# Projections with the split activations streamed side by side: 512-column and 256-column matmuls in place of three of 256

## What is computed

```python
def conv_ffn(h, w_in, conv_w, conv_b, w_out):        # w_in 2048 x 11264, w_out 5632 x 2048
    u = h @ w_in
    u = conv_general_dilated(u, conv_w, causal, depthwise, width 3) + conv_b
    x1, x2 = jnp.split(u, 2, axis=-1)
    return (gelu(x1) * x2) @ w_out

# in rwkv7_time_mix, each of the three weights 2048 x 2048
    r = xr @ w_r
    k = xk @ w_k
    v = xv @ w_v
```

## Time and profile before

| | |
|---|---|
| median of 3 executions | 3236.29 us (3229.45 to 3247.82) |
| span of the profiled execution | 3236.4 us |
| up projection of the first ConvFFN | 508.6 us |
| up projection of the second ConvFFN | 508.8 us |
| r, k, v projections | 95.1, 93.9 and 95.0 us |
| pieces of weights made (all phases) | 792 |

### The profile page before, as it was taken

The page is one execution under the profiler, slowest core; times in us unless marked ns, Lnnn a source line. Parts: engine busy times, 40 slices in busy tenths (PEclk is TensorE's granted clock), DMA queues, the critical chain, the costliest instruction groups (busy, mean ns, idle before and its releaser), DMA issues.

```text
span 3236.4 us, 69175 instructions
## 1 busy us (share of the span) xinstructions
PE 2869.6 (89%) x27134; PEld 2794.3 (86%) x27134; DVE 2113.4 (65%) x2599; ACT 1468.9 (45%) x1994; POOL 151.8 (5%) x160
## 2 busy tenths in 40 slices
PE   2399999899999999985999677778788999999998
PEld 2399998899999998975999677667688999999998
DVE  6777777866666666678453598989537666665434
ACT  0143333466666633338453232322245666665333
POOL 0000000000000000000000221221000000000000
PEclk8599999899999999997999888989899999999999
DMA  8788788655555578872565444545344555555553
GB/s 298 250 280 278 273 275 283 234 180 183 182 181 181 182 242 279 289 225 73 162 194 169 145 145 151 161 132 166 112 146 144 181 181 181 182 182 178 184 171 125
DMA packets 489769, 628.05 MB, mean 194 GB/s; under 512 B 26392, under 2 KB 434824, under 8 KB 489352
## 3 DMA queue, kind: packets, MB, share of 16 engines
q1 hardware_dynamic: 485568, 622.62, 58.7%
q10 hardware_dynamic: 4040, 3.07, 0.3%
HBM read 623.50 MB, written 2.10 MB: 193 GB/s over the span
## 4 chain that ended last, share of the span: by engine, by line
PE 71%; DVE 15%; DMA 6%; issue 4%; ACT 3%; DVEq 0%; ACTq 0%; SPq 0%
PE ps L1709 62%; DVE macc L1135 5%; PE ps L1884 5%; DMA raw<-in_ffn_w_out 4%; DVE wlo L1114 2%; ACT whi L722 1%; PE ps L1730 1%; DVE nrm L1492 1%; PE ps L1721 1%; DVE mx L1433 1%; DVE pinv L1502 1%; DVE ut L1599 1%; PE ps L1794 1%; PE ps L1792 1%; DMA crow<-in_ffn_conv_b 0%
## 5 line engine op out<-in xcount | busy, mean ns | idle before, releaser
L1114 DVE TENSOR_TENSOR wlo<-raw,whi 128x1024 fp32r<-128x1024 f32 x792 | 968.1, 1227 | 841.2 <-ACT whi L722 840.0
L1709 PE MATMUL ps<-xs,whi 128*128 128x256 f32 x7680 | 1408.4, 286 | 27.8 <-DVE xs L1198 16.6
L722 ACT ACTIVATE whi<-raw 128x1024 fp32r<-128x1024 f32 x792 | 831.8, 1057 | 1053.1 <-PE ps L1709 648.0
L1709 PEld LDWEIGHTS ps<-xs,whi 128*128 128x128 f32 x7680 | 1218.0, 195 | 33.3 <-issue 21.5
L1709 PE MATMUL ps<-xs,wlo 128*128 128x256 f32 x3840 | 1097.2, 286 | 0.0
L1709 PEld LDWEIGHTS ps<-xs,wlo 128*128 128x128 f32 x3840 | 748.7, 195 | 0.0
L1709 PE MATMUL ps<-act,whi 128*128 128x256 f32 x3840 | 709.1, 287 | 39.8 <-DVE wlo L1114 39.4
L1709 PEld LDWEIGHTS ps<-act,whi 128*128 128x128 f32 x3840 | 609.9, 195 | 45.4 <-DVE wlo L1114 45.2
L1709 PE MATMUL ps<-act,wlo 128*128 128x256 f32 x1920 | 549.1, 286 | 0.0
L1135 DVE SCALAR_TENSOR_TENSOR macc<-raw,cact,macc 128x1024 f32<-128x1024 f32 (+1 forms) x364 | 449.4, 1235 | 11.0 <-DMA raw<-in_mod_w 3.2
L1709 PEld LDWEIGHTS ps<-act,wlo 128*128 128x128 f32 x1920 | 374.8, 195 | 0.0
(11 more groups left out here) (231 smaller groups left out, 2722.0 us busy)
## 6 DMA issues: line engine op xcount, KB each, us to landing
raw<-in_ffn_w_in SPq DMA_DIRECT2D x352, 512.0 KB, 3.4
raw<-in_mod_w SPq DMA_DIRECT2D x288, 512.0 KB, 4.7
raw<-in_ffn_w_out SPq DMA_DIRECT2D x176, 512.0 KB, 4.6
raw<-in_fox_w_in SPq DMA_DIRECT2D x96, 512.0 KB, 5.8
raw<-in_mod_w SPq DMA_DIRECT2D x128, 384.0 KB, 5.0
raw<-in_fox_w_out SPq DMA_DIRECT2D x32, 512.0 KB, 7.2
raw<-in_rwkv_w_r SPq DMA_DIRECT2D x32, 512.0 KB, 3.5
raw<-in_rwkv_w_k SPq DMA_DIRECT2D x32, 512.0 KB, 3.5
```

The source lines that it names most:

```text
L722: sc.activation(whi[:, half, :, :].rearrange("p k n -> p (k n)"), slots[slot], ACT.Copy).then_inc(w_hi, 1)
L1114: v.tensor_tensor(wlo[:, half, :, :].rearrange("p k n -> p (k n)"), slots[slot], whi[:, half, :, :].rearrange("p k n -> p (k n)").bitcast( ...
L1709: last = pe.matmul(ps[bank][:, m * S:m * S + S], lhs, rhs, start=begin and m == 0 and h == 0, stop=end and h == 2, skip_group_check=True)
```

## The change

PSUM banks 0 and 1 become the tensor `duo[0]`, banks 2 and 3 `duo[1]`. Instead of two tiles side by side in one bank, each of the two tiles `m` gets a bank of its own. High weights stream high and low activations as one operand of 512 columns: columns 0 to 255 of the bank then hold the high-by-high sum, columns 256 to 511 the high-by-low sum. Low weights stream the 256 high activations into columns 0 to 255 as before. So 3 matmuls with 3 weight loads become 2 with 2, and the number of columns that are streamed stays at 768. On leaving PSUM, ACT copies the right halves of both banks to `ub`, `rk` or `vfm` (`side`), and DVE then adds the left halves to that (`joined`, or `result` in the r, k, v stages). ACT's two `vb` operations now read `ub` instead of PSUM and wait for DVE. The last lap's `joined` stands on DVE ahead of the first early piece of the down projection.

```diff
-        ps = [ctx.enter_context(nc.psum_tensor(f"ps{b}", [P, 512], F32)) for b in range(8)]
+        duo = [ctx.enter_context(nc.psum_tensor(f"ps{b}{b + 1}", [P, 2, 512], F32)) for b in (0, 2)]
+        ps = [duo[b // 2][:, b % 2, :] for b in range(4)]
+        ps += [ctx.enter_context(nc.psum_tensor(f"ps{b}", [P, 512], F32)) for b in range(4, 8)]
...
 # ACT, up_proj
+                def side(i, half):
+                    sc.wait_ge(w_used, ph.weight(i, 4 * half + 3))
+                    sc.activation(ub[:, 2 * half:2 * half + 2, 2:S + 2], duo[half][:, :, S:2 * S],
+                                  ACT.Copy).then_inc(*s["s2" if half else "s1"].inc("side"))
                 def taps(i, half, steps_):
-                    sc.wait_ge(w_used, ph.weight(i, 4 * half + 3))
-                    src = ps[half][:, :].rearrange("p (m t) -> p m t", m=2)
-                    sc.activation(ub[:, 2 * half:2 * half + 2, 2:S + 2], src, ACT.Copy).then_inc(*steps_.inc("u"))
+                    sc.wait_ge(*s["u2" if half else "u1"].at("u", i))
                     for m in range(2):
-                        sc.activation(vb[:, 2 * half + m, :], src[:, m, :], ACT.Identity,
+                        sc.activation(vb[:, 2 * half + m, :], ub[:, 2 * half + m, 2:S + 2], ACT.Identity,
...
                     for w in range(8):
                         hi_new(ph, i, w)
+                        if w == 0 and not first:
+                            taps(i - 1, 0, s["a1"])
                         if w == 1 and not first:
                             gelu(i - 1)
                         if w == 3 and not first:
+                            side(i - 1, 1)
+                        if w == 4 and not first:
                             taps(i - 1, 1, s["a2"])
-                        if w == 5 and not first:
+                        if w == 6 and not first:
                             product_hi(i - 1)
                         if w == 7:
                             if first:
                                 sc.wait_ge(*s["z"].at("zero"))
-                            else:
-                                sc.wait_ge(*s["v2"].at("prod", i - 1))
-                            taps(i, 0, s["a1"])
+                            side(i, 0)
                 laps(UP_ITERS, body)
+                taps(UP_ITERS - 1, 0, s["a1"])
                 early(ph_down[n], 0)
                 gelu(UP_ITERS - 1)
+                side(UP_ITERS - 1, 1)
                 taps(UP_ITERS - 1, 1, s["a2"])
...
 # ACT, rkv_body: result() becomes side()
-                    sc.activation(dst, ps[s][:, :].rearrange("p (m t) -> p m t", m=2),
-                                  ACT.Copy).then_inc(*rk_a[j].inc(f"s{s}"))
+                    sc.activation(dst, duo[s][:, :, S:2 * S], ACT.Copy).then_inc(*rk_a[j].inc(f"s{s}"))
...
 # DVE, up_proj
+                def joined(i, half):
+                    v.wait_ge(*s["s2" if half else "s1"].at("side", i))
+                    u = ub[:, 2 * half:2 * half + 2, 2:S + 2]
+                    v.tensor_tensor(u, duo[half][:, :, 0:S], u, ALU.add).then_inc(*s["u2" if half else "u1"].inc("u"))
...
-                    pieces(ph, i, None if first else {0: lambda: conv(i - 1, 0, s["a1"], s["v1"]),
-                                                      4: lambda: second_half(i - 1), 6: lambda: product_lo(i - 1)})
+                    hooks = {7: lambda: joined(i, 0)}
+                    if not first:
+                        hooks |= {1: lambda: conv(i - 1, 0, s["a1"], s["v1"]), 3: lambda: joined(i - 1, 1),
+                                  5: lambda: second_half(i - 1), 6: lambda: product_lo(i - 1)}
+                    pieces(ph, i, hooks)
                 laps(UP_ITERS, body)
                 conv(UP_ITERS - 1, 0, s["a1"], s["v1"])
+                joined(UP_ITERS - 1, 1)
                 early(ph_down[n], 0)
                 second_half(UP_ITERS - 1)
...
 # DVE, r, k and v
+                def result(i, s):
+                    tiles = ds(i * 4 + 2 * s, 2)
+                    dst = vfm[:, tiles, :] if j == 2 else rk[:, tiles, j, :]
+                    v.wait_ge(*rk_a[j].at(f"s{s}", i))
+                    v.tensor_tensor(dst, duo[s][:, :, 0:S], dst, ALU.add).then_inc(*rk_v[j].inc(f"s{s}"))
...
+                    hooks[7] = lambda: result(i, 0)
+                    if not first:
+                        hooks[3] = lambda: result(i - 1, 1)
...
                 laps(4, rkv_body)
-            v.wait_ge(w_used, ph_rkv[2].weight(3, 7))
-            v.wait_ge(*rk_a[2].at("s1", 3))
+                result(3, 1)
+            for j in range(3):
+                v.wait_ge(*rk_v[j].at("s1", 3))
...
 # PE
+            def paired_slab(ph, i, w0_, bank, src, ready=None):
+                for q in range(4):
+                    w = w0_ + q
+                    half = ph.half(w)
+                    pe.wait_ge(raw_done, ph.done(i, ph.w_at[w]))
+                    for k in range(PIECE_KT):
+                        if ready and k % 2 == 0 and ready(2 * q + k // 2):
+                            pe.wait_ge(*ready(2 * q + k // 2))
+                        kt = PIECE_KT * q + k
+                        for m in range(2):
+                            pe.matmul(ps[bank + m][:, :], whi[:, half, k, m * P:m * P + P],
+                                      src[:, kt, :, :].rearrange("p u s -> p (u s)"), start=kt == 0, stop=False,
+                                      skip_group_check=True)
+                            last = pe.matmul(ps[bank + m][:, 0:S], wlo[:, half, k, m * P:m * P + P], src[:, kt, 0, :],
+                                             start=False, stop=kt == KT - 1, skip_group_check=True)
+                    last.then_inc(w_used, 1)
...
-                    slab(ph_up[n], i, 0, 4, 0, xs, ready=lambda r_: norm[2 * n + 1]["v"].at(f"lo{r_}"))
-                    slab(ph_up[n], i, 4, 4, 1, xs)
+                    paired_slab(ph_up[n], i, 0, 0, xs, ready=lambda r_: norm[2 * n + 1]["v"].at(f"lo{r_}"))
+                    paired_slab(ph_up[n], i, 4, 2, xs)
...
-                    slab(ph_rkv[j], i, 0, 4, 0, mix_to(3 + j), ready=lambda r_: mix_lo.at("lo", 8 * (3 + j) + r_))
-                    slab(ph_rkv[j], i, 4, 4, 1, mix_to(3 + j))
+                    paired_slab(ph_rkv[j], i, 0, 0, mix_to(3 + j), ready=lambda r_: mix_lo.at("lo", 8 * (3 + j) + r_))
+                    paired_slab(ph_rkv[j], i, 4, 2, mix_to(3 + j))
```

More of the change, by code:

```diff
@@ L425, in trunk @@
         rk_a = [steps(f"rk_a{n}", "s0 s1") for n in range(3)]
+        rk_v = [steps(f"rk_v{n}", "s0 s1") for n in range(3)]
         hd_pe = steps("hd_pe", "lora n2 bon")
@@ L986, in _, with side @@
             for j in range(3):
-                def result(i, s):
+                def side(i, s):
                     sc.wait_ge(w_used, ph_rkv[j].weight(i, 4 * s + 3))
-                    dst = vfm[:, ds(i * 4 + 2 * s, 2), :] if j == 2 else rk[:, ds(i * 4 + 2 * s, 2), j, :]
-                    sc.activation(dst, ps[s][:, :].rearrange("p (m t) -> p m t", m=2),
-                                  ACT.Copy).then_inc(*rk_a[j].inc(f"s{s}"))
+                    tiles = ds(i * 4 + 2 * s, 2)
+                    dst = vfm[:, tiles, :] if j == 2 else rk[:, tiles, j, :]
+                    sc.activation(dst, duo[s][:, :, S:2 * S], ACT.Copy).then_inc(*rk_a[j].inc(f"s{s}"))
                 def rkv_body(i, first):
@@ L1003, in rkv_body @@
                         if w == 3 and not first:
-                            result(i - 1, 1)
+                            side(i - 1, 1)
                         if w == 5 and j < 2:
@@ L1008, in rkv_body @@
                         if w == 7:
-                            result(i, 0)
+                            side(i, 0)
                 laps(4, rkv_body)
-                result(3, 1)
+                side(3, 1)
             def sigmoids(i):
@@ L1459, in both @@
                             what(4 + j, i * 2 + g, g)
-                    pieces(ph_rkv[j], i, {2: lambda: both(mixed_sum), 6: lambda: both(mixed_lo)} if j < 2 else None)
+                    hooks = {2: lambda: both(mixed_sum), 6: lambda: both(mixed_lo)} if j < 2 else {}
+                    hooks[7] = lambda: result(i, 0)
+                    if not first:
+                        hooks[3] = lambda: result(i - 1, 1)
+                    pieces(ph_rkv[j], i, hooks)
                 laps(4, rkv_body)
-            v.wait_ge(w_used, ph_rkv[2].weight(3, 7))
-            v.wait_ge(*rk_a[2].at("s1", 3))
+                result(3, 1)
+            for j in range(3):
+                v.wait_ge(*rk_v[j].at("s1", 3))
             v.wait_ge(lvl_in, 16)
```

4 lines of the change are left out of this document (3 added, 1 removed).

## The result

| | before | after |
|---|---|---|
| median of the executions (range) | 3237.5 us (3229.5 to 3247.8) | 3192.5 us (3188.2 to 3207.6) |
| ratio | | 0.9873 (0.9855 to 0.9892) |
| span of the profiled execution | 3236.4 us | 3190.7 us |
| matmuls | 27134 | 23550 |

The change gains 1.3%, 45 us. The direction was forecast; the size was half of it, and the range (3138 to 3193) has the median at its very edge. The profiled execution of after took 3192.5 us at a span of 3190.7, so some 1.8 us lie around a span, which my sum had left out.

The account below looks back on a forecast made before the run. The prediction took PE's pace to bound five stages, 1301.4 us or 40% of the span. The span of 3236.4 us, less 85.2 for the pairs, plus 2.0 at the stage ends, gave 3153 us, range 3138 to 3193.

Parts of the forecast that it names:

- What bounds the kernel: Both up projections and the r, k, v stages, 1301.4 us or 40% of the span, go at PE's pace.
- Part 1, the pair: In PE-bound stages, 512 plus 256 columns take 336 ns against 360; 3549 groups gain 24 ns each, 85.2 us.
- float32 record: Profile record of a plain float32 matmul, taken as a 512-column stream at 215 ns; nearest row for the new matmul.
- rival (a): PE's floor goes with the columns: 512 cost 2 x 113, the pair 347 ns; time 3192 us, chance 0.14.
- no toll once a stream lasts that long: Claim from 256-column starts at 1.2 GHz, 213 ns, that fp32r adds nothing of its own to the 512-column matmul.
- The bound: If the excess of 7 to 13 ns went with the columns, the pair would take 347 to 360 ns.
- Part 2: Inside the laps DVE and ACT keep up; the 112 additions, 76 us of DVE, cost nothing.
- Part 3: At the up projections' ends, DVE's addition delays PE's second down piece: 1.0 us per ConvFFN, 2.0 in all.
- a pair of 340 ns: Slow end of the expected 333 to 340 ns for 512 plus 256 columns, put at 3169 us.
- rival (b): On PE the price is nearly all streaming: 512 columns cost 238, a pair 358 ns; 3229 us, chance 0.05.
- (c): Both matmuls of the pair on PE are freed of the floor, 324 ns; time 3111 us, chance 0.07.
- (d): Slower: ACT's in-order waits for DVE's additions cost 2.5 us in each up lap, 110 us; 3263 us, chance 0.04.

Follow-up runs that it names:

- split3: The changed kernel with its 512-column matmul cut in two again, so three matmuls of 256 columns; 3236.0 us, ratio to the kernel before 0.9999.
- mb3: Bench of PE alone with the operands moved about in SBUF; 512 columns took 227 ns at word 0, 236 one word on, 233 two words on.
- mb4: Bench of PE alone with more places of moving operand and weights; 256 columns took 120.0 ns with neither moved, 117.8 with either one moved 16 words.
- before16: The kernel before the change with its three tiles of moving operands 64 bytes further against the weights' tiles; 3203.9 us, ratio 0.9906.
- mb1: Bench of PE alone, runs of 96 matmuls from resident tiles without DVE, ACT or DMA work; fp32r took 227 ns for 512 columns, 120 for 256.
- mb2: Second bench of PE alone, with more column lengths and repeats; 448 columns took 202.7 ns, 384 took 173.3, and 224, 192 and 160 all 111.7.
- ends: The changed kernel with DVE's low tile of the first down piece ahead of its last up-projection addition; 3200.6 us, ratio to the kernel before 0.9878.

## Why the prediction was wrong

- **What bounds the kernel**: right. The five stages go at PE's pace before and after; `split3` shows that nothing else enters.
- **Part 1, the pair**: this step failed. I put the 512-column matmul at 216 ns by the float32 record of the same stream length. It measures 227 alone and 230 to 241 in the pair; with 112 to 120 for the short one the pair is 346.7 or 353.3, not 336. That record differs "in type alone", I wrote, and the type was the point: bf16 has 216 for 512 columns in the same bench in which fp32r has 227. Why the float32 record has 215 isn't shown. A guess is that it is two passes over 256 columns, which ask for each word at half the pace; nothing here tests it. The row that did carry over was the other one of the earlier trace rows, 113 ns for 256 fp32r columns with a narrow weight load, which I had given to rival (a) at 0.14: 2 x 113 + 120 = 347, 3192 us. The mean gain was 41 us / 3549 = 11.6 ns, where I had 24. That I took the 213 ns of the earlier trace rows for "no toll once a stream lasts that long" was the slip: those rows show no toll at the pace of 1.2 GHz, and say nothing of a long stream at 2.4.
- **The bound** of that step, 347 to 360, had it; the range followed it only to 3193.
- **Part 2**: right. DVE's additions took 0.683 us as in the earlier trace rows, DVE's busy time in an up projection rose from 313.5 us to 338 and 339, and no stage has a wait of PE inside its laps.
- **Part 3**: right in kind, and 0.9 us of the addition at each end where I had 1.0. In all, 2 us were forecast and 4 measured in the first profile, 1.4 and 1.9 in the two others of the same kernel. The clock had been left out of it.
- **Two small slips in the sums**, which change nothing: a pair of 340 ns gives 3236.4 - 71 + 2 = 3167 us, not 3169, and the 358 of rival (b) are a gain of 2 ns a group, 7 us, not 9.
- **The rivals**: (a) gives the time to a fraction of a microsecond, and that is in part luck. Its mechanism was half of it: fp32r columns do have a price of their own, at least 113.3 ns for 256 in every place, but more of it hangs on the place of the operands and on the start. Its sum of 227 and 120 isn't how the pair is made: a narrow weight load takes 7 ns from a short matmul among its equals and nothing from the pair. And 3192.5 is the median of four executions whose stages draw their levels; the same kernel had 3201.3 and 3201.7 in the later runs. (b), (c) and (d) did not come; no level under 340 ns a group was seen in any of the runs, and in the stages of the changed kernel each weight load still starts when the matmul before its own does, as in the earlier trace rows.

What stays open: what in SBUF or PE makes an fp32r stream at full clock slower than its columns, and why by place; why a stage keeps the level in which it starts, and what of its start decides. The runs show that other engines aren't needed for it, and that the places of both operands and the start matter; they show no mechanism.

## What to carry to other kernels

Price a merged matmul from a row of the same type at the same clock level; a row of another type with the same stream length was a lower bound here (216 ns for 227), not a price. Where fp32r matmuls run back to back at full clock, the place of the moving tile against the weight tile is worth a try before any restructuring: 64 bytes gave three quarters of what the restructuring gave. And two stages with the same instructions and different lengths are a finding, to be read from the starts of their matmuls before it is put down to noise.

## What the runs showed of the hardware

- fp32r matmuls of 256 columns with full weights run at 113.3 to 123 ns at full clock, most often at 120.0, 117.8 or 113.3, by the places of moving operand and weights and by the start (`mb3`, `mb4`, `before16`); 512 columns at 227 to 237. bf16 matmuls have 109 and 216 (`mb1`).
- A pair of 512 and 256 columns takes 346.7 ns with weight loads 128 wide and also with one of the two 16 wide (`mb1`).
- A moving operand in fp32r with a stride of two words costs double: 451 ns for 512 columns against 227 (`mb3`).
- Matmuls of 128 to 224 columns with 128-wide fp32r weights all cost 112 ns (`mb1`, `mb2`).
- A stage of identical matmul pairs held one of two paces (346.7 or 353.3 ns) for all its 490 or 499 us in each of three profiled executions, and the mixture was another in each.
- A standstill of PE of 3.6 us was followed by 13 and by 24 matmuls at the 1.2 GHz level (`ends`). One of 2.8 us was followed by 13 in the changed kernel when the up projection ahead of it was at the high level (four times in four), and by none when it was at the low one (twice in two); by what this comes isn't shown.
